# First norm of a two-block transformer kernel: sums of squares taken from the tokens as loaded, factors spread by small products, first weights split beside it

## What is computed

```
h = concat(meta, x)                                  # 528 x 1024
hn = h / sqrt(mean(h*h over the 1024 features) + 1e-6) * norm_pre[0]
z = hn @ hy_w_in + hy_b_in                           # 1024 -> 8192, in 32 chunks of 256 columns
```

## Time and profile before

| what | value |
| --- | --- |
| median of 3 runs | 2703.68 us (2698.56 to 2704.16) |
| the profiled execution: its own time, its span | 2704.6 us, 2702.6 us |
| PE busy, share of the span | 2381.8 us, 88% |
| DVE, ACT, POOL busy | 1696.0 us, 1305.8 us, 821.0 us |
| mean granted PE clock | 0.941 of 2.4 GHz |
| first matmul of the projections starts at | 59.23 us |

### The profile page before, as it was taken

How to read it: one execution, slowest core, us unless ns; L and a number is a source line. 1 busy time by engine, 2 the same in 40 slices (tenths; PEclk the granted TensorE clock), 3 DMA queues, 4 the chain that set the end, 5 groups by cost and what they waited for, 6 DMA issues and landing times.

```text
span 2702.6 us, 38622 instructions
## 1 busy us (share of the span) xinstructions
PE 2381.8 (88%) x15931; PEld 2116.5 (78%) x15931; DVE 1696.0 (63%) x2598; ACT 1305.8 (48%) x2125; POOL 821.0 (30%) x506
## 2 busy tenths in 40 slices
PE   4999997889899899999998898888887874999994
PEld 3999996888899888899997776667666763777873
DVE  3455445778753766666666668846566425888885
ACT  3444334344432556556555333542344212888884
POOL 1211113554531222222221120213010113777672
PEclk8999998899999999999998999998898976999997
DMA  4223420111042222222222331123111432778773
GB/s 146 79 80 89 134 79 32 32 32 32 13 137 78 59 76 71 70 76 70 77 72 63 80 92 43 47 72 109 40 44 41 127 110 95 285 281 288 283 267 147
DMA packets 226600, 273.43 MB, mean 101 GB/s; under 512 B 42088, under 2 KB 194249, under 8 KB 213754
## 3 DMA queue, kind: packets, MB, share of 16 engines
q1 hardware_dynamic: 211914, 262.54, 31.0%
q0 software_dynamic: 14512, 8.45, 1.0%
HBM read 283.24 MB, written 31.05 MB: 116 GB/s over the span
## 4 chain that ended last, share of the span: by engine, by line
PE 53%; DVE 22%; ACT 11%; POOL 6%; issue 5%; DMA 2%; SPq 1%; DVEq 0%; POOLq 0%; ACTq 0%
PE ps L92 16%; PE ps L94 15%; PE ps L93 15%; ACT whi L98 2%; DVE prods L1145 2%; ACT sp L114 1%; DVE wlo L102 1%; PE ps L1821 1%; DVE fsum L972 1%; DVE p L2116 1%; POOL xg L3885 1%; DVE work L2715 1%; DVE m L2713 1%; ACT X L114 1%; PE ps L1831 1%
## 5 line engine op out<-in xcount | busy, mean ns | idle before, releaser
L92 PE MATMUL ps<-hn_h,whi 128*128 128x264 f32 (+2 forms) x2256 | 690.3, 306 | 38.5 <-POOL wlo L102 30.1
L94 PE MATMUL ps<-hn_h,wlo 128*128 128x264 f32 (+2 forms) x2256 | 673.0, 298 | 0.0
L93 PE MATMUL ps<-hn_l,whi 128*128 128x264 f32 (+2 forms) x2256 | 673.0, 298 | 0.0
L92 PEld LDWEIGHTS ps<-hn_h,whi 128*128 128x128 f32 x2256 | 430.0, 191 | 67.7 <-issue 36.9
L94 PEld LDWEIGHTS ps<-hn_h,wlo 128*128 128x128 f32 x2256 | 430.3, 191 | 12.1
L93 PEld LDWEIGHTS ps<-hn_l,whi 128*128 128x128 f32 x2256 | 430.4, 191 | 9.5 <-issue 0.2
L102 POOL TENSOR_TENSOR wlo<-wraw,whi 128x2048 fp32r<-128x2048 f32 (+1 forms) x46 | 167.8, 3647 | 547.9 <-ACT whi L98 547.9
L98 ACT ACTIVATE whi<-wraw 128x2048 fp32r<-128x2048 f32 (+1 forms) x164 | 260.2, 1587 | 61.4 <-PE ps L94 61.3
L102 DVE TENSOR_TENSOR wlo<-wraw,whi 128x2048 fp32r<-128x2048 f32 (+1 forms) x118 | 250.4, 2122 | 49.7 <-ACT whi L98 49.5
L732 DVE SCALAR_TENSOR_TENSOR c<-ub,vec,c 128x528 f32<-128x528 f32 x48 | 45.3, 944 | 140.4 <-ACT c L114 140.4
L114 ACT ACTIVATE ub<-ps,vec 128x528 f32<-128x528 f32 x48 | 33.7, 702 | 165.5 <-PE ps L94 165.5
(11 more groups left out here) (772 smaller groups left out, 6758.3 us busy)
## 6 DMA issues: line engine op xcount, KB each, us to landing
wraw<-in_w_gate_up SPq DMA_DIRECT2D x33, 1024.0 KB, 7.3
wraw<-in_hy_w_in SPq DMA_DIRECT2D x32, 1024.0 KB, 5.6
wraw<-in_da_w_in SPq DMA_DIRECT2D x64, 512.0 KB, 4.2
ex_raw<-in_w_gate_up SPq DMA_DIRECT2D x31, 1024.0 KB, 6.6
ex_raw<-in_w_down SPq DMA_DIRECT2D x17, 1024.0 KB, 6.6
wraw<-in_w_down SPq DMA_DIRECT2D x15, 1024.0 KB, 7.0
wraw<-in_w_in SPq DMA_DIRECT2D x14, 1024.0 KB, 5.4
wraw<-in_hy_w_out SPq DMA_DIRECT2D x8, 1024.0 KB, 8.2
```

The source lines that it names most:

```text
L92: e.matmul(out, lhsT=l[0], rhs=r[0], start=start, stop=False)
L93: e.matmul(out, lhsT=l[0], rhs=r[1], start=False, stop=False)
L94: return e.matmul(out, lhsT=l[1], rhs=r[0], start=False, stop=stop)
```

## The change

- **Loads**: SP issues weight chunk 0 right behind x and meta, ahead of the vectors.
- **Order on PE**: transposes of x blocks 0 to 4 come first, in three pairs of banks; the vectors are transposed before block 5 (into bank 4), and six small fp32 products before block 6 (`tensor_factors`).
- **Copies to hT**: DVE takes both pieces of each block (400 and 128 columns); ACT none.
- **Sums of squares**: ACT squares the five loaded token tiles (tokens on partitions, 1024 features along) with an accumulator, which gives one number for each token in `rc[128, 5]`; one root over `rc`, and one reciprocal by DVE. A product of column j of `rc`, broadcast over 128 columns as stationary operand, with the identity puts the factors of token block j on all partitions, in pair 3 of the banks.
- **Norm**: the scaled block k is written by DVE to a pair of PSUM banks (pairs 2 and 1 in turn) instead of `ntmp`; ACT takes the high part from there, and DVE all eight low parts. The reads of the factors are from PSUM too.
- **First weights**: ACT splits chunk 0 right after the root, ahead of the norm's high parts; POOL takes its low part there, as it has no low parts of the norm any more.
- **Biases** `hb` and `mb` are worked out by DVE after the norm, and ACT waits for them before it splits chunk 1.
- **Projections**: in all 64 units the loop over k is now the outer one and the loop over halves the inner one; unit 0 waits for each k as it comes.
- **Tables**: ACT runs a dummy root at the start.

```diff
     def sync_inputs(e, w):
         for j in range(4):
             e.dma_start(xin[j][:], I["x"][0, 128 * j:128 * j + 128, :]).then_inc(*land("x"))
         e.dma_start(xin[4][0:16, :], I["meta"]).then_inc(*land("x"))
+        sync_weights(e, w, 0)
...
+    def tensor_vectors(e, w):
+        w.wait_ge("v")
+        w.wait_ge("in.vec", "x", 2)
+        for b in range(3):
+            n = VUSED[b]
+            t = e.transpose(bank[4][:, 128 * b:128 * b + n], vst[b][0:n, :], ident[0:n, 0:n])
+        t.then_inc(*mark("in.pe", "vec"))
+
+    def tensor_factors(e, w):
+        w.wait_ge("n0.vec", "r")
+        for j, (a, b) in enumerate(BLOCKS):
+            for i in range(2):
+                c, d = max(a, 264 * i), min(b, 264 * i + 264)
+                if c < d:
+                    t = e.matmul(pairs[3][:, i, c - 264 * i:d - 264 * i], lhsT=rc[:, j:j + 1].broadcast_to([128, 128]),
+                                 rhs=ident[:, c - a:d - a], start=True, stop=True)
+        t.then_inc(*mark("n0.pe", "r"))
...
         for k in range(8):
-            pr = pairs[k % 4]
...
+            pr = pairs[k % 3]
+            if k == 5:
+                tensor_vectors(e, w)
+            elif k == 6:
+                tensor_factors(e, w)
+            if k >= 3:
+                w.wait_ge("in.vec", "x", k - 3)
+            if k == 5:
+                w.wait_ge("in.vec", "vec")
...
+        act(e, rc[:, 4:5], eps6, ACT.Sqrt).then_inc(*mark("in.act", "table"))
+        w.wait_ge("in.act", "table")
+        w.wait_ge("x")
+        for j in range(5):
+            n = 128 if j else 16
+            act(e, xsq[j][0:n, :], xin[j - 1 if j else 4][0:n, :], ACT.Square, accum=rc[0:n, j:j + 1]).then_inc(*mark("n0.act", "sq"))
+        w.own("n0.act")
+        act(e, rc[:], rc[:], ACT.Sqrt, bias=eps6, scale=1.0 / D).then_inc(*mark("n0.act", "sqrt"))
...
+    def vector_x(e, w, k):
+        w.wait_ge("in.pe", "x", k)
+        e.tensor_copy(hT[:, k, 0:400], pairs[k % 3][:, 0, 0:400]).then_inc(*mark("in.vec", "xa", k))
+        e.tensor_copy(hT[:, k, 400:528], pairs[k % 3][:, 1, 0:128]).then_inc(*mark("in.vec", "x", k))
+
+    def vector_inputs(e, w):
+        for k in range(5):
+            vector_x(e, w, k)
+        w.wait_ge("n0.act", "sqrt")
+        e.reciprocal(rc[:], rc[:]).then_inc(*mark("n0.vec", "r"))
+        vector_vectors(e, w)
+        vector_x(e, w, 5)
+        vector_x(e, w, 6)
...
+    def scaled_in(k):
+        return pairs[2 - k % 2][:, :, 0:264]
+
     def scalar_norm0(e, w):
-        scalar_rstd(e, w, "n0", lambda k: hT[:, k, :], T, 8, eps6, r0, bank[6:8], x_there)
-        scalar_norm(e, w, "n0", T, ntmp)
...
+        scalar_weights(e, w, 0)
+        for k in range(8):
+            w.wait_ge("n0.vec", "scaled", k)
+            hi_part(e, halves(hn_h[:, k, :]), scaled_in(k)).then_inc(*mark("n0.act", "hi", k))
+
+    def vector_scaled(e, w, k):
...
+        e.scalar_tensor_tensor(scaled_in(k), halves(hT[:, k, :]), V["pre0"][:, k:k + 1], pairs[3][:, :, 0:264], ALU.mult,
+                               ALU.mult).then_inc(*mark("n0.vec", "scaled", k))
 
     def vector_norm0(e, w):
...
+        vector_scaled(e, w, 0)
+        vector_x(e, w, 7)
+        vector_scaled(e, w, 1)
+        for k in range(8):
+            w.wait_ge("n0.act", "hi", k)
+            lo_part(e, halves(hn_l[:, k, :]), scaled_in(k), halves(hn_h[:, k, :])).then_inc(*mark("n0.vec", "lo", k))
+            if k + 2 < 8:
+                vector_scaled(e, w, k + 2)
+        vector_biases(e, w)
 
     def gpsimd_norm0(e, w):
-        gpsimd_norm(e, w, "n0", T, ntmp)
+        lo_weights(e, w, "pool", 0)
...
-            for i in range(2):
-                a, b = 264 * i, 264 * i + 264
-                for k in range(8):
-                    normed(w, "n0", k)
+            for k in range(8):
+                normed(w, k)
+                for i in range(2):
+                    a, b = 264 * i, 264 * i + 264
                     t = mm3(e, pr[:, i, 0:264], (wh[:, k, c], wl[:, k, c]), (hn_h[:, k, a:b], hn_l[:, k, a:b]), k == 0, k == 7)
...
         for kind, x, step in HY:
             pr = pairs[step % 4]
+            w.wait_ge("in.vec", "mb")
```

More of the change, by code:

```diff
@@ L397, in build @@
     vst = [sb(f"vst{i}", [128, 128], F32, FREE + 20480 + 512 * i) for i in range(3)]
+    xsq = [sb(f"xsq{i}", [128, D], F32, FREE + 22016 + 4096 * i) for i in range(5)]
+    rc = sb("rc", [128, 5], F32, FREE + 67584)
     def sync_inputs(e, w):
@@ L408, in gpsimd_inputs @@
         e.memset(ident[:], 0.0).then_inc(*mark("in.pool", "zero"))
+        e.memset(eps6, 1e-6).then_inc(*mark("in.pool", "eps"))
+        e.memset(rc[:, 0:1], 1.0).then_inc(*mark("in.pool", "rc"))
         e.memset(ones[:], 1.0).then_inc(*mark("in.pool", "ones"))
@@ L438, in scalar_inputs, with vector_vectors, vector_biases @@
         hi_part(e, identr[:], ident[:]).then_inc(*mark("in.act", "identr"))
-        for k in range(8):
-            w.wait_ge("in.pe", "x", k)
-            act(e, hT[:, k, 0:400], pairs[k % 4][:, 0, 0:400], ACT.Copy).then_inc(*mark("in.act", "x", k))
-    def vector_inputs(e, w):
+        w.wait_ge("in.pool", "rc")
+        act(e, rc[:, 4:5], eps6, ACT.Sqrt).then_inc(*mark("in.act", "table"))
[6 more added lines that the diff above has]
+        act(e, rc[:], rc[:], ACT.Sqrt, bias=eps6, scale=1.0 / D).then_inc(*mark("n0.act", "sqrt"))
+    def vector_vectors(e, w):
+        w.wait_ge("in.pe", "vec")
         for b in range(3):
             n = VUSED[b]
-            w.wait_ge("in.pe", "vec", b)
-            e.tensor_copy(vec[:, 128 * b:128 * b + n], bank[b][:, 0:n]).then_inc(*mark("in.vec", "vec", b))
-        w.own("in.vec")
+            e.tensor_copy(vec[:, 128 * b:128 * b + n], bank[4][:, 128 * b:128 * b + n]).then_inc(*mark("in.vec", "vec"))
+    def vector_biases(e, w):
         ts(e, hb, V["b_in"][:, 48:64], 0.5, None, ALU.mult).then_inc(*mark("in.vec", "hb"))
@@ L759, in sync_hyena @@
                 w.wait_ge("keep", "out")
-                normed(w, "n0", 6)
-                normed(w, "n0", 7)
+                normed(w, 6)
+                normed(w, 7)
                 for d, src in [(zT, C["zT"])] + [(fw[i], I[f"hy_f_w{i + 1}"][0]) for i in range(3)]:
@@ L4165, in tensor @@
         tensor_inputs(e, w)
-        tensor_norm0(e, w)
         tensor_hyena(e, w)
```

33 lines of the change are left out of this document (11 added, 22 removed).

## The result

The changed kernel took 2679.93 us (median of 3 runs, 2677.94 to 2680.71) against 2703.68 us: ratio 0.9916, 95% interval 0.9894 to 0.9939, so 24 us less; 2674 was forecast. The profiled execution has a span of 2678.7 us and took 2680.7. Over all eleven runs the median is 2676.8.

What follows compares the result with a forecast made beforehand. An unbroken chain of start work bounds the kernel until PE's first projection at 59.23 us, then PE. Unit 1 ends at 43.1 instead of 73.07, 29.9 less: 2704.6 to 2674.7, less 0.9 to the median, 2674; range 2668 to 2682.

Steps and rivals of the forecast that it cites:

- x has landed: Start of the chain: PE waits for x and meta, landed at 10.4 us; the weight chunk behind is charged nothing.
- Blocks 0 to 4 and the root: Five transpose blocks on PE at 1.26 us, done at 16.7; ACT's squares and root beside them, ready at 16.6.
- Block 5: PE waits for DVE's reciprocal and vector copies until 18.5, then transposes block 5 in 1.26 us, to 19.8.
- Factors: Six small fp32 products on PE before block 6: 1.5 us, to 21.3 (1.9 at the upper price).
- Norm: DVE's scalings and low parts after the transposes: 1.5 us a block, second scaling ending at 26.0, last low part at 36.5.
- Units 0 and 1: First projections on PE: unit 0 follows the norm, ending at 37.3; unit 1 takes 5.85 us, to 43.1 instead of 73.07.
- The splits: First weights: POOL's chunk 0 split done at 23.1, 2.9 us early; chunk 1's at 41.4, 1.7 us before unit 2.
- Half clock: Rival: PE's clock falls to half around the gap from 23.9 to 26.7, costing 2.8 us: 2676.6 us; chance 0.11.
- DVE slower at writing banks: Rival: DVE slower writing PSUM, or root, vectors or chunk 1 late: +2 to +6 us, 2676 to 2680; chance 0.11.
- shut out by POOL: Rival: DVE's copies from PSUM wait from 18.5 until POOL's split ends at 23.1: +4.6 us, 2678.4; chance 0.03.
- The loop order: Other 62 units charged nothing; rival: 896 more bank changes make it slower, 2728 us at 60 ns each; chance 0.03.
- What the start gains, the end gains: Stages after the start wait for each other's results, not a clock time, so the 29.9 us reaches the end.

Runs made afterwards that it cites:

- all eleven runs: The changed kernel, unaltered, on three occasions: 2679.93 us (3 runs), 2673.7 us (4 runs) and 2676.2 us (4 runs).
- the further version: Changed kernel with units 0 and 1 multiplied together block by block and the factor products before block 5 of the transposes: 2676.0 us (6 runs), ratio 0.9903.
- experiment 3: Changed kernel with ACT's high part of weight chunk 0 moved behind the norm's eight high parts, so both splits come late: 2690.7 us against 2676.2 beside it.
- the delayed form: Changed kernel with an idle wait before the first load (POOL fills a tile eight times): 2691.2 us (5 runs) and, on another occasion, 2689.3 us (4 runs).
- the second occasion: The changed kernel, unaltered, run a second time: 2673.7 us (4 runs), ratio 0.9892.

## Why the prediction was right, and what it missed

- *Unit 1 within 0.1 us*: the price of a block of transposes, the covers and the order of events were right. That the figure is so close is luck in part: the factors took 1.1 us more than forecast, and an earlier block 5 and a faster norm gave it back.
- *x has landed*: forecast 10.4, PE starts at 10.32. The weight load behind it cost x nothing, and the vectors came in time: PE waited for their copies by DVE (0.93 us), not for their landing.
- *Blocks 0 to 4 and the root*: 16.7 forecast, 16.67 measured for PE. The root was done at 15.9, not 16.6, since a square followed the last after 1.04 us here, not 1.18.
- *Block 5*: forecast to end at 19.8, ended at 19.4.
- *Factors*: the term that was mis-sized, 1.5 us forecast, 2.56 measured. I took 9.79/32 = 0.31 us as the price of one fp32 product, but the 32 instructions were 16 products: each fp32 product that isn't a transpose runs as two matmul instructions. The six products here are twelve instructions, 0.21 us each (2.56/12), at the half level of the clock; the further version, at the full level, took 1.54 us for the same twelve. The upper price of 1.9 did not cover it.
- *Norm*: 1.42 us a block, forecast 1.5. The second scaling ended 0.2 us later than forecast; from there on the norm gave back more than that: last low part at 36.1, forecast 36.5.
- *Units 0 and 1*: 43.01, forecast 43.1.
- *The splits*: POOL's ran from 17.8 to 22.3 (forecast to end at 23.1), and no DVE instruction waited for it: those beside it were copies from banks, at their usual 0.57 and 0.28 us. The small reciprocal had ended at 17.6, and the first scaling began at 24.0. PE wanted the split at 27.0; the 2.9 us of cover in the prediction were counted from 26.0, by its own 26.7 they were 3.6. Chunk 1's low part ran from 38.54 to 40.83, under unit 1. Both covers held, and the late split shows what the first is worth, 13 us. The Trainium skill (SBUF — State Buffer, "Who interferes with whom") says that a DVE instruction with two SBUF inputs contends with a GpSimd instruction that reads SBUF, and that one with at most one such input does not. Three rows bear it out: the copies from banks beside POOL, 4.91 us for a low part with two SBUF inputs beside it in experiment 3 (2.29 alone), and 1.44 us for the scaling above.
- *Half clock*: the rival came about, without its price. Products of unit 0 came every 0.22 us from 27 to 30.8 us, the pace of the half level, and 0.12 after; the sign "granted clock 1.0 from 24 to 43" was wrong. The price I gave (2.8 us) supposed that the clock would stay down into unit 1. It rose while PE was still following DVE, and there the half speed was hidden: six products took about 1.35 us, a block of DVE 1.42. Nor had it fallen in the gap before: the factors were already at the half level.
- *DVE slower at writing banks; shut out by POOL*: neither; 0.77 us, and no wait.
- *The loop order*: charged with nothing, feared as a loss. It is a gain of 2.7 us in the projections, shown in both directions. The Trainium skill (TensorE: Matmul & The Clock Gate, "A second HAM failure mode: psum-queue depth-cycling") tells of a kernel whose clock swung while it cycled through banks, PE being idle for short times between its groups of matmuls. Here nothing of it was seen: PE was busy for 374 of the 379 us from 31 to 410, the granted clock was 1.00 throughout, and units that follow one another directly came 5.80 us apart.
- *"What the start gains, the end gains"* is the step that holds only in part. The marks promise 30.1 + 2.7 = 32.8 us; the eleven runs give 26 to 27, and the first three 24. Shown is that the stages after the projections vary from one execution to the next by up to 8 us with the same instructions, that the kernel before passes a delay on in full (9.2 of 9.6 us), and that by the median runs the rest is longer with the new start: 2262.6 to 2268.4 us in the three occasions of the changed kernel against 2258.1 to 2259.7, and the delayed form took 4 to 8 us more than its delay. What failed is the reason given for it, that the later stages only wait for each other's results: their length is not fixed by that, since PE's clock level in them differs. The places that could be read one by one (4.92 us for 24 products instead of 2.6 to 3.0, and a fall of the clock that costs 1.5 us) are stretches at the half level. Open stays how much of the loss is the clock's, and why the kernels with the new start meet more of it. A different phase in which DVE and POOL meet finds no support: their time of working together does not go with the rest.

So the time forecast (2674) lies nearest to the second occasion. All three lie within the wide range (2668 to 2682); the first, 2679.9, lies outside the forecast's own range of 2670 to 2678. That the medians of the other two fall so near is luck in part: a loop-order gain that was not counted (2.7 us) lay against an assumption of full passing on.

## What to carry to other kernels

Work that waits for the last of a stage can often follow it block by block, and then even a half-speed engine is hidden under the one it follows; look for the engine that makes the blocks and let nothing else stand before it. Statistics over features are cheap where tokens lie on partitions: five squares with an accumulator and a small root and twelve small matmul instructions took the place of 32 large ones, a 3.46 us reciprocal and a table load on the path. When a change is worth 1% or less, read it at marks close to it (here repeatable within 1 us) as well as in the total, whose later stages may vary by more than the change. Take a total from the median of many runs and not from one profile: the changed kernel with the old order had a rest of 2259.5 us in its profile, the fastest of its five runs, and 2264.9 by their median. And before a difference of a few us is put down to an edit, compare the clock level of the stretch in both profiles.

## What the runs showed of the hardware that was not expected

**A granted clock of 1.00 may only mean that there is no record yet.** The window view of the changed kernel says 1.00 for 27 to 29 us (sixth number after the span's):

```profile
27.00:29.00 2.00, 2.00 (x9) 2.00 (x10) 1.96 (x4) 0.61 (x1) 0.00 (x0) 1.00 1.10 465
```

but the timeline of PE shows products 0.22 us apart there, and 0.12 apart later:

```profile
27.57 0.42 PE L94 MATMUL ps<-hn_h,wlo 128*128 128x264 f32 x1
27.79 0.42 PE L92 MATMUL ps<-hn_h,whi 128*128 128x264 f32 x1
...
36.65 0.28 PE L92 MATMUL ps<-hn_h,whi 128*128 128x264 f32 x1
36.77 0.28 PE L93 MATMUL ps<-hn_l,whi 128*128 128x264 f32 x1
```

In the further version, whose clock is recorded from 16.6 us on, the same stretch reads 0.50. Weight loads tell it too: those of the factors took 333 ns each, as the slowest of the products with ones before (186 to 337), where those at the full level take 187 to 190:

```profile
L437 PEld LDWEIGHTS ps<-ident,rc x12: 333/333/337, 19.0 to 21.4; 128*128 128x128 f32 x12
```

So the factors, too, ran at the half level. In the further version the same loads, with a recorded clock of 1.00, took:

```profile
L437 PEld LDWEIGHTS ps<-ident,rc x12: 186/190/191, 17.5 to 18.7; 128*128 128x128 f32 x12
```

A block of transposes took 0.75 us there instead of 1.26. The 1.26 us in the kernel before, from which the prediction took its price, is thus the price at the half level, though the view says 1.00 there too.

**The clock level of later stages differs between executions of the same or nearly the same instructions**, and this moved single places by 1.5 us and by some 2 us: 24 products took 2.6 to 3.0 us or 4.92.

**Two accumulation groups in turn, with the same weights, are a little cheaper than one after the other**: 5.80 against 5.85 us for 48 products, and 366.7 against 369.4 us for the projections, 0.9 ns a product, in every kernel with that order and in none without. Whether the banks or the weights do it was not tested.
